# A one-core hybrid decoder block: the bonus product's place, its filler, the first experts' loads and the last bias products

## The reference, cut to what matters

```
xn   = rms_norm(x);  proj = xn @ w_in
o_att  = block-sparse causal attention (8 heads x 64)
o_rwkv = RWKV-7 time mixing (8 heads x 64):
    per token:  state = state * w_t + (state @ -kk_t) b_t + v_t k_t ;  o_t = state @ r_t
    bonus = sum(r * k * r_k) * v ;   (groupnorm(o) + bonus) * g
h    = x + concat(o_att, o_rwkv) @ w_out
xn2  = rms_norm(h);  top 4 of 32 experts, softmax over their logits
y    = sum over the 4:  gate * (((clip(xn2 @ w_up + b_up) + 1) * swish(min(xn2 @ w_gate + b_gate))) @ w_down + b_down)
out  = rms_norm(h + y)
```

## Time and profile before

| | us |
|---|---|
| median of 3 runs (lowest, highest) | 1573.56 (1573.19, 1576.79) |
| the profiled execution's own time | 1572.38 |
| its span, first to last instruction | 1570.6 |
| TensorE busy in it | 1514.7 |
| VectorE busy in it | 1324.3 |
| ScalarE busy in it | 1087.7 |
| GpSimd busy in it | 579.6 |

### The profile page before, as it was taken

The page is one execution under the profiler, slowest core; times in us unless marked ns, Lnnn a source line. Parts: engine busy times, 40 slices in busy tenths (PEclk is TensorE's granted clock), DMA queues, the critical chain, the costliest instruction groups (busy, mean ns, idle before and its releaser), DMA issues.

```text
span 1570.6 us, 29528 instructions
## 1 busy us (share of the span) xinstructions
PE 1514.7 (96%) x10609; PEld 1248.0 (79%) x10609; DVE 1324.3 (84%) x1459; ACT 1087.7 (69%) x1319; POOL 579.6 (37%) x370
## 2 busy tenths in 40 slices
PE   7999987889999999999999999999999999999997
PEld 6877767776888778888888888888888888888884
DVE  4246456556699899999999999999999999999996
ACT  4245431104477888788888878888888888888874
POOL 7000313101030322543444555554455445345442
PEclk9999999999999999999999999999999999999999
DMA  7321110001699999999999999999999999999994
GB/s 243 95 68 41 40 42 3 4 4 68 247 369 368 407 373 388 391 389 388 380 376 389 393 398 387 394 386 372 388 393 385 394 391 391 380 383 393 392 388 145
DMA packets 81279, 464.41 MB, mean 296 GB/s; under 512 B 11642, under 2 KB 12854, under 8 KB 33072
## 3 DMA queue, kind: packets, MB, share of 16 engines
q1 hardware_dynamic: 71424, 438.68, 70.9%
q0 software_dynamic: 9104, 24.52, 6.9%
q10 hardware_dynamic: 672, 0.07, 0.0%
HBM read 449.16 MB, written 23.13 MB: 301 GB/s over the span
## 4 chain that ended last, share of the span: by engine, by line
PE 85%; DVE 10%; DMA 2%; issue 1%; ACT 1%; POOL 1%; POOLq 0%; ACTq 0%; SPq 0%; DVEq 0%
PE banks L385 70%; DVE expert_w_lo L325 5%; PE banks L1859 5%; PE banks L1952 1%; DMA expert_w_raw<-in_moe_w_up_dram 1%; PE banks L2057 1%; PE banks L2107 1%; PE banks L1936 1%; DMA up_bias_rows<-in_moe_b_up_dram 1%; PE banks L2122 1%; POOL up_bias_rows L761 1%; PE banks L2125 0%; PE banks L2134 0%; PE banks L2533 0%; PE banks L2399 0%
## 5 line engine op out<-in xcount | busy, mean ns | idle before, releaser
L325 DVE TENSOR_TENSOR expert_w_lo<-expert_w_raw,expert_w_hi 128x1024 fp32r<-128x1024 f32 x764 | 911.0, 1256 | 25.6 <-ACT expert_w_hi L320 24.9
L320 ACT ACTIVATE expert_w_hi<-expert_w_raw 128x1024 fp32r<-128x1024 f32 x764 | 750.4, 1056 | 34.1 <-DMA expert_w_raw<-in_moe_w_down_dram 26.4
L385 PE MATMUL banks<-expert_w_hi,x_block_T_hi 128*128 128x512 f32 x1008 | 395.7, 393 | 0.7 <-DVE expert_w_lo L325 0.5
L385 PE MATMUL banks<-expert_w_lo,x_block_T_hi 128*128 128x512 f32 x1008 | 392.6, 389 | 0.0
L385 PE MATMUL banks<-expert_w_hi,x_block_T_lo 128*128 128x512 f32 x1008 | 392.1, 389 | 0.0
L753 POOL COPY scatter_gates<-slot_gate 128x1 f32 x23 | 189.0, 8216 | 220.8 <-DMA y_sums<-y_block,scatter_rows 220.8
L385 PEld LDWEIGHTS banks<-expert_w_hi,x_block_T_hi 128*128 128x128 f32 x1008 | 189.4, 188 | 40.6 <-issue 1.7
L385 PEld LDWEIGHTS banks<-expert_w_lo,x_block_T_hi 128*128 128x128 f32 x1008 | 189.2, 188 | 39.8
L385 PEld LDWEIGHTS banks<-expert_w_hi,x_block_T_lo 128*128 128x128 f32 x1008 | 189.4, 188 | 38.0
L385 PE MATMUL banks<-expert_w_hi,h_block_T_hi 128*128 128x512 f32 x528 | 209.3, 396 | 3.1 <-DVE expert_w_lo L325 2.6
L385 PE MATMUL banks<-expert_w_lo,h_block_T_hi 128*128 128x512 f32 x528 | 205.9, 390 | 0.0
(11 more groups left out here) (403 smaller groups left out, 1926.4 us busy)
## 6 DMA issues: line engine op xcount, KB each, us to landing
expert_w_raw<-in_moe_w_up_dram SPq DMA_DIRECT2D x128, 1024.0 KB, 9.2
expert_w_raw<-in_moe_w_down_dram SPq DMA_DIRECT2D x128, 1024.0 KB, 10.2
expert_w_raw<-in_moe_w_gate_dram SPq DMA_DIRECT2D x126, 1024.0 KB, 10.2
w_raw<-in_w_in_dram SPq DMA_DIRECT2D x24, 512.0 KB, 4.0
residual<-in_x_dram SPq DMA_DIRECT2D x8, 512.0 KB, 5.1
w_raw<-in_w_out_dram SPq DMA_DIRECT2D x8, 512.0 KB, 3.2
staged_raw<-in_moe_w_gate_dram SPq DMA_DIRECT2D x2, 1024.0 KB, 5.9
y_sums<-residual SPq DMA_DIRECT2D x4, 512.0 KB, 6.1
```

The source lines that it names most:

```text
L320: act.activation(self.hi[:, k % self.nhl, 0:width], self.raw[:, slot, 0:width], ACT.Copy)\
L325: dve.tensor_tensor(self.lo[:, k % self.nhl, 0:width], self.raw[:, (k - self.staged) % self.nraw, 0:width], self.hi[:, k % self.nhl, 0:wid ...
L385: last = pe.matmul(o, lhs, rhs, start=start and t == 0, stop=stop and t == 2, skip_group_check=preset)
```

## The change

The constants and the function of the filler are removed. On DVE, front_bonus(n+1) now stands before back_maps(n). PE gets 20 products of ident by 32 columns of ident into bank 7 before the first transposes. On SP, blocks 1 to 7 are written out, g_fin goes behind the loads of block 5 and bd4 behind those of block 7; block 2's bias rows now come as one row and are spread by POOL, like those of the blocks after it, and the counts of bias_spread shift by two. In the tail the bias products of tiles 0 to 2 are issued first, half by half, so that neighbours in the program lie in different groups of 32 rows; tile 3's stand before its own sums, since pair 0 is in use until the last block's y has been read. On DVE the scalings of tile 0 stand behind the additions of tile 2 and those of tiles 1 to 3 behind all additions.

```
-    WARM, WARM_N = (7, 7, 6, 0), 160
...
             def bias_load(i, rows, name, e, landed):
-                if isinstance(i, int):
+                if isinstance(i, int) and i < 2:
...
-            block_loads(1, 1, 0)
-            sp.dma_start(g_fin[:, :], t_in["norm_final_g"].partition_broadcast(P)).then_inc(S("late_params_in"), 16)
+            for i in range(1, 8):
+                block_loads(i, i, i - 1)
+                if i == 5:
+                    sp.dma_start(g_fin[:, :], t_in["norm_final_g"].partition_broadcast(P)).then_inc(S("late_params_in"), 16)
             for q in range(4):
                 sp.dma_start(bd4[32 * q:32 * q + 32, :], t_in["moe_b_down"][0]).then_inc(S("late_params_in"), 16)
-            block_loads(2, 2, 1)
-            with sp.Fori(0, NE - 3) as it:
-                block_loads(it + 3, it + 3, it + 2)
+            with sp.Fori(0, NE - 8) as it:
+                block_loads(it + 8, it + 8, it + 7)
...
-                pool.wait_ge(S("bias_spread"), i * 2 + which - 5)
+                pool.wait_ge(S("bias_spread"), i * 2 + which - 3)
...
-                spread = not (isinstance(i, int) and i < 3)
+                spread = not (isinstance(i, int) and i < 2)
...
-                back_maps(n)
                 if more:
                     front_bonus(n + 1)
+                back_maps(n)
...
-                if tt >= 2:
-                    scaled_out(tt - 2, 0)
-                    scaled_out(tt - 2, 1)
-            for tt in (TT - 2, TT - 1):
+                if tt == TT - 2:
+                    scaled_out(0, 0)
+                    scaled_out(0, 1)
+            for tt in range(1, TT):
                 for f in range(2):
                     scaled_out(tt, f)
...
             pe.wait_ge(S("consts_ok"), 3)
+            for k in range(20):
+                pe.matmul(bank[7][:, 0:32], ident[:, :], ident[:, 0:32], start=True, stop=True)
...
-            def keep_warm(count):
-                for k in range(count):
-                    pe.matmul(bank[IV[0]][:, 256:256 + WARM_N], head_ones[:, :], SCM[:, 0:WARM_N], start=True, stop=True)
...
-                keep_warm(WARM[n])
...
+            for f in range(2):
+                for tt in range(TT - 1):
+                    down_bias(tt, f)
             pe.wait_ge(S("rows_ok"), TT + 1)
             for tt in range(TT):
-                down_bias(tt)
                 for f in range(2):
+                    if tt == TT - 1:
+                        down_bias(tt, f)
                     last_sum(tt, f)
```

More of the change, by code:

```diff
@@ L2528, in last_down, with down_bias @@
                     last.then_inc(w_used, 1)
-            def down_bias(tt):
+            def down_bias(tt, f):
                 rows = slice(32 * tt, 32 * tt + 32)
-                for f in range(2):
-                    pe.matmul(last_bank(tt)[:, 512 * f:512 * f + 512], gmapT[rows, :], bd4[rows, 512 * f:512 * f + 512],
-                              start=True, stop=False, skip_group_check=True)
+                pe.matmul(last_bank(tt)[:, 512 * f:512 * f + 512], gmapT[rows, :], bd4[rows, 512 * f:512 * f + 512],
+                          start=True, stop=False, skip_group_check=True)
             def last_sum(tt, f):
```

8 lines of the change are left out of this document (4 added, 4 removed).

## The result

The changed kernel took 1562.52 us (median of 8 runs, 1557.47 to 1564.73) beside 1572.97 for the kernel before (8 runs, 1568.10 to 1576.79): ratio 0.9934, 95% interval 0.9920 to 0.9948. Measured again, it gave 1561.20 against 1572.47, ratio 0.9933 (0.9913 to 0.9953). So it is faster, by 10.4 and 11.3 us, where 18.2 were forecast; 1562.52 lies 1 us above the range that was given. The profiled execution took 1563.11, with a span of 1561.4. I go through the stages of the working, in the order of time.

What follows compares the result with a forecast made beforehand. TensorE's threefold products bound the kernel (70% of the chain, busy from 500 to 1500 us), so gains come only before and after: 12.5 + 3.7 + 2.0 + 0 = 18.2; 1573.56 - 18.2 = 1555.4 us, range 1552 to 1561.5.

Steps and rivals of the forecast that it cites:

- Recurrence: Tiles n=0 to 2: filler removed and PE's wait for the bonus gone, gain 12.5 us, bounds 8 to 13.5.
- Rival B: Recurrence: without filler more low-clock stretches come; fifteen us of them cost 6, giving 1561; chance 0.13.
- Rival C: Recurrence: bonus isn't what PE waited for, or only the filler's time returns: 5.7 instead of 12.5, 1562; chance 0.06.
- Tail: End of kernel: bias products of three tiles run together, DVE then the path; gain 3.7 us, bounds 0 to 4.2.
- First expert blocks: Less DMA before weights of blocks 2 and 3, fewer PE waits on low parts: gain 2.0 us, bounds 0 to 3.1.
- rival F: First expert blocks: block 2's up broadcast is held, block 3's stays held, gate broadcast costs too: 1558.4; chance 0.05.
- Head: Start of kernel: 20 added products, half at full and half at low clock, net 0; bounds gain 0.4, loss 2.
- second case: Head: all 40 instructions at low clock end at 11.6, 3.8 late; twice 0.8 won back, 1.9 to 2.2 lost.
- base of the forecast: Whole kernel before: profiled 1572.38, runs' median taken as 1.2 above it, so 1573.56 us.

Runs made afterwards that it cites:

- wide head: Kernel after with 128 columns instead of 32 in each of its 20 head products: 1556.89 (0.9903); measured again 1558.25 (0.9905).
- pair without head: Kernel after without its 20 head products: 1562.11, ratio 0.9934; the same with the filler put back: 1559.96, ratio 0.9919.
- ten products added: Kernel after with 10 head products of 128 columns, plus ten 32-column products: ahead of the expert loop 1561.91 (0.9935); in the tail 1566.73 (0.9972).
- wide head with the filler: Kernel after with 20 head products of 128 columns and the filler put back in the recurrence: 1564.49, ratio 0.9949.
- wide head alone: Kernel before with only 20 head products of 128 columns added ahead of its first transposes: 1575.00, ratio 1.0019.

## Why the prediction was right or wrong

**Recurrence: right in its mechanism, and close in its number partly by luck.** Forecast 12.5. The eight traces with the bonus ahead and no filler (and nothing added) have 81.97 to 84.57, mean 83.3; the five with neither edit 94.63 to 96.41, mean 95.4: a gain of 12.1. The 10.2 of the first pair of traces comes from a low value of the one kind and a high one of the other. Of the parts, the filler measures 6.6 alone (95.4 to 88.8) where 5.7 was taken, and the order alone 9.3 in one trace where 6.8 was; together they give less than the sum.

Two things that the working left out lie behind these numbers, and they work against each other. The first is the granted clock: every one of the five traces of the old order with the filler has one stretch at 1.2 GHz within the recurrence (in the first trace 267.7 to 271.1, of which the window of the earlier trace rows caught only a part), the two of the old order without the filler have two, and none of the thirteen of the new order has any. One such stretch is worth some 1.7 us, so moving the bonus brought 6.8 and about 1.7. The second is the short pauses: with their time taken off, the recurrence is 91.3 on average in the old order with the filler and 77.3 in the new order without it, 14.0 apart, which is near 12.5 + 1.7; the pauses, 4.1 before and 6.0 now, took back 1.9. The subtraction is an estimate, as not every pause need lie on the path.

Rival B asked whether the clock suffers without the filler. The full pair (wide head with and without it) says no: 6.2 us in time, 6.6 and 6.1 in the stage (89.86 against 83.30 and 83.77). In the pair without head it is less, 1.2 and 3.8 (85.80 against 84.57 and 81.97), so the filler's price goes with the rest of the program. In the new order there is no low stretch with it or without it. In the old order it did spare one of two, and still cost more than that. Rival C is out too: the idle time before L2164 is gone.

**Tail: right in its mechanism.** Forecast 3.7, in the profiled execution 3.6. Over the traces the new tail is 13.9 to 16.1 (16.2 with ten products added), against 17.96 before, so up to 1.8 us of the 3.7 are given back. Where it is longest, DVE waits for the residual that returns from y_sums; in the wide head with the filler:

```profile
DVE residual L1847 <- DMA residual<-y_sums: 3.4, 2, 2.3
```

The kernel before has no such wait in its trace; its additions came later, and waited for PE. This DMA is what is late next, and the working did not name it.

**First expert blocks: right.** Forecast 2.0; nine traces with the new loads and without the wait have a mean of 1106.9, five with the old ones 1109.3: 2.4. Weight latency and waits moved as described, block 2's broadcasts took 2.21 and 1.30 us, so rival F did not happen.

**Head: the step that failed.** The working took half of the 40 instructions at full clock and half at low, "I take that, 0", with 2 us as the worst. All 40 ran at the low rate, as in its second case, whose "twice 0.8 is won back" was wrong as well: the first 24 transposes behind them took 4.46 us, 0.19 each, since the rate doubled only at 15.0 (at 17.4 in the second trace), so nothing came back, and the loss was the whole 3.9. The head column says 19.0 with the narrow products (four traces) and 15.7 without any (nine): 3.3. The 15.21 of the kernel before was the earliest of its kind; that is 0.5 of the 3.9.

**The sum.** By the stage means: 12.1 + 2.4 + tail 3.1 (17.96 to 14.84, over the new tails without added products) - 3.3 = 14.3, against 10.4 and 11.3 measured. Of the 7.8 us by which the gain fell short of 18.2, the mis-sized head accounts for 3.3 to 3.9 and the tail for 0.6; what the recurrence lacks (0.4) the first blocks have more. The base of the forecast (1573.56, where 8 runs gave 1572.97) was 0.6 too high, and so the time missed by 7.1 only. Some 3 to 4 us stay open by the first measurement, and 2 to 3 by the second. They are of the size by which executions of one program differ. One source of such differences can be read: the stage behind the recurrence has 86.21 in the first trace of the kernel after and 84.16 in the second, and the first has a stretch at the low clock there that the second has not. Of the twenty traces only this one and the wide head alone have one in that stage. Its cause is open.

```profile
356.30:359.70 3.40, 3.40 (x35) 1.97 (x34) 0.42 (x1) 1.15 (x2) 0.00 (x0) 0.50 0.00 0
```

**What the 2x2 of head and filler hid.** Removing either seemed worth nothing (the head from after, 1562.5 to 1562.1; the filler from before, ratio 1.0006). Both removals gain in their own stage (3.3 and 6.6 us); both shortened the program ahead of the last block by the same 40 rows, and paid 6.5 to 6.8 us there (1115.8 against 1109.3, 1113.7 against 1106.9): the wait of 4.4, and the low rate behind it. The stage behind the recurrence gives back 1.2 (83.0 in all four). In the change as made, the head's 40 rows stand in for the filler's 40; that this kept the wait away was luck, as the working did not know of it. Shown are the dependence on the place and the price; that it is the fetch of instructions is argued, from where the q8 packets lie and from the inputs being there.

Still open in part: why the head alone costs 5.3 us when narrow and 3.0 when wide, by the ratios, when the head stage has 3.3 and nothing. In the one trace of each, the pauses in the recurrence sum to 5.4 and 6.5 us, against 1.8 in that of the kernel before, and the wide one has the low stretch behind it. Of the programs with 10649 rows, the two with the new order are 4 us slower in the recurrence than the two with 10609 rows and filler (90.1 against 86.0); the pauses differ by 5.0 (7.4 against 2.4). So the place of the code seems to act there too, but no run here separates it from the rest.

## What to carry to other kernels

Work put in to raise the clock must be over before the real inputs arrive, and its length is to be priced at the low rate; here four times the columns cost nothing per instruction, and the full rate came at 7.3 us instead of 15.0 and 17.4. When an edit removes instructions and the time does not move, compare the traces stage by stage, far from the edit too, at each loop exit above all: the place of the code may have taken what was gained, and the test for it is the same number of instructions added elsewhere ahead of that place. Compare stages over several traces of each kind, since one low-clock stretch or a few short pauses in a single execution (1.7 us for such a stretch, and 4.6 to 7.7 us of pauses in kernels of one kind, here) can hide an edit of this size.

## What the hardware showed beyond what I expected

Forty instructions of 32 columns, back to back for 8.7 us, left TensorE at the low rate; with 128 columns the rate doubled 4.3 us after their start, at the same 0.21 us each until then. The column of granted clock shows 1.00 in these first microseconds in either case.

Entering code behind a loop stopped TensorE for 4.3 to 4.5 us in six traces of six whose program has 20 or 40 rows of PE fewer ahead of that place than the kernel after, and in none of the fourteen others; twenty rows more ahead of it removed the wait, twenty behind it did not. TensorE's 94 pauses of 0.7 to 1.6 us with no releaser in the recurrence all stand 1.0 to 1.8 us ahead of a packet of its instruction queue.
